# Two attentions with fewer waits, and the reciprocal of a block's sum moved behind the next block's maximum

## What is computed

```python
def one_block(qi):                       # 128 queries of one head against all 1024 keys
    s = jnp.einsum('bqkgd,bskd->bkgqs', qi, k, preferred_element_type=jnp.float32) * scale
    p = jax.nn.softmax(s, axis=-1)
    return jnp.einsum('bkgqs,bskd->bqkgd', p.astype(v.dtype), v)
```

```python
s = jnp.where(kpos[None, :] <= qpos[:, None], s, -jnp.inf)
prob = jax.nn.softmax(s, axis=-1)
outs.append(jnp.einsum('bhqk,bhkd->bhqd', prob.astype(v.dtype), v[:, :, :q1]))
```

## Time and profile before

| | us |
|---|---|
| median of 3 runs | 2623.56 |
| lowest and highest | 2619.59, 2625.0 |
| span of the profiled execution | 2619.9 |
| PE busy of the span | 2539.2 (97%) |
| DVE busy | 1587.0 (61%) |
| ACT busy | 1233.5 (47%) |
| POOL busy | 1132.0 (43%) |
| first attention, back of step 2 to back of step 62 | 188.07 |

### The profile page before, as it was taken

One profiled execution on the slowest core, in us unless ns is written; L12 is line 12 of the kernel. 1 busy time (PEld: TensorE's weight loads), 2 busy tenths in 40 slices (PEclk: granted clock), 3 DMA queues, 4 the chain that ended last, 5 costly groups with the idle time before them and its releaser, 6 DMA issues.

```text
span 2619.9 us, 33861 instructions
## 1 busy us (share of the span) xinstructions
PE 2539.2 (97%) x12946; PEld 2112.9 (81%) x12946; DVE 1587.0 (61%) x2413; ACT 1233.5 (47%) x1858; POOL 1132.0 (43%) x754
## 2 busy tenths in 40 slices
PE   5999999999999999999999999999999999999998
PEld 3788788777888888878788888888888888888886
DVE  7654889578555566575833366666666666655333
ACT  4343888445444443333533345543656656652132
POOL 0222434437878774444487334233322222235233
PEclk8999999999999999999999999999999999999999
DMA  6134000432222126553233322222111111157342
GB/s 271 65 121 129 1 1 1 142 101 83 94 77 92 73 100 226 192 177 109 107 113 121 121 73 89 81 69 93 57 53 53 49 49 57 60 206 279 146 185 97
DMA packets 84465, 275.89 MB, mean 105 GB/s; under 512 B 9392, under 2 KB 9520, under 8 KB 84304
## 3 DMA queue, kind: packets, MB, share of 16 engines
q1 hardware_dynamic: 84304, 273.71, 29.8%
HBM read 219.54 MB, written 54.13 MB: 104 GB/s over the span
## 4 chain that ended last, share of the span: by engine, by line
PE 81%; DVE 10%; ACT 5%; issue 2%; POOL 1%; DMA 0%; DVEq 0%; SPq 0%; ACTq 0%; POOLq 0%
PE ps L609 12%; PE ps L611 11%; PE ps L610 11%; PE ps L977 7%; PE ps L978 7%; PE ps L979 7%; PE ps L848 5%; PE ps L829 4%; PE ps L1034 3%; PE ps L1036 3%; PE ps L1035 3%; DVE wf L3047 2%; PE ps L805 2%; PE ps L806 2%; DVE st L2573 1%
## 5 line engine op out<-in xcount | busy, mean ns | idle before, releaser
L3374 POOL TENSOR_TENSOR hl<-raw,hl 128x1024 fp32r<-128x1024 f32 x161 | 403.6, 2509 | 929.9 <-ACT hl L1393 929.9
L609 PE MATMUL ps<-ht,hl 128*128 128x512 f32 x1552 | 633.7, 408 | 10.5 <-DVE ht L2444 5.4
L611 PE MATMUL ps<-ht,hl 128*128 128x512 f32 x1552 | 608.4, 392 | 0.0
L610 PE MATMUL ps<-ht,hl 128*128 128x512 f32 x1552 | 608.2, 392 | 0.0
L609 PEld LDWEIGHTS ps<-ht,hl 128*128 128x128 f32 x1552 | 293.6, 189 | 71.3 <-issue 6.2
L611 PEld LDWEIGHTS ps<-ht,hl 128*128 128x128 f32 x1552 | 293.0, 189 | 63.7
L610 PEld LDWEIGHTS ps<-ht,hl 128*128 128x128 f32 x1552 | 294.0, 189 | 54.2 <-issue 1.7
L3451 POOL TENSOR_SCALAR wf<-wf,st 128x1024 f32<-128x1024 f32 (+2 forms) x192 | 167.9, 874 | 343.1 <-DVE st L2581 287.4
L1393 ACT ACTIVATE hl<-raw 128x1024 fp32r<-128x1024 f32 x163 | 171.4, 1053 | 182.2 <-PE ps L1036 66.5
L2384 DVE TENSOR_TENSOR ps<-ps,wf 128x512 f32<-128x512 f32 x116 | 80.8, 697 | 152.1 <-PE ps L979 151.9
L829 PEld LDWEIGHTS ps<-cst,wf 128*128 128x128 f32 x1088 | 126.6, 141 | 56.2 <-issue 34.4
(11 more groups left out here) (287 smaller groups left out, 5298.5 us busy)
## 6 DMA issues: line engine op xcount, KB each, us to landing
raw<-in_wst SPq DMA_DIRECT2D x243, 512.0 KB, 4.0
wf<-scratch_rows SPq DMA_DIRECT2D x32, 512.0 KB, 5.0
scratch_g<-wf SPq DMA_DIRECT2D x22, 512.0 KB, 2.6
wf<-scratch_g SPq DMA_DIRECT2D x44, 256.0 KB, 4.4
wf<-in_xT SPq DMA_DIRECT2D x16, 512.0 KB, 8.0
htf<-in_wst SPq DMA_DIRECT2D x16, 512.0 KB, 15.4
scratch_ys<-wr SPq DMA_DIRECT2D x16, 512.0 KB, 4.8
ht<-scratch_ys SPq DMA_DIRECT2D x32, 256.0 KB, 6.0
```

The lines of the kernel that those rows point to most:

```text
L609: self.op.matmul(out, wh, xh[:, c], start=(j == 0), stop=False)
L610: self.op.matmul(out, wh, xl[:, c], start=False, stop=False)
L611: t = self.op.matmul(out, wl, xh[:, c], start=False, stop=(j == kt - 1))
L3374: self.op.tensor_tensor(K.hl[:, u * 2048 + 1024:u * 2048 + 2048], K.raw[:, i % 3 * 1024:(i % 3 + 1) * 1024], hi.bitcast(F32), ALU.subtract ...
```

## The change

- DVE, first attention: in step s the order top(s+2), turn(s), soft(s+2), back becomes top(s+2), soft(s+1), turn(s), back. The reciprocal of block s+1 is thus issued one step later than before, behind the maximum of block s+2.
- PE, first attention: in scores(s+2), from s = 0 on, the last of the four matmuls gets a wait for `weighed` of block s. turn(s), which follows, waits for the same label already.
- Waits left out in both attentions, since another wait that stays, or the new one, includes them: on PE `top` ahead of the scores (first attention) and `phi` ahead of turn and back; on ACT `top` (causal) or `scores` (first), the first half of `turn` of block g-4, and `weighed` of block g-16; on DVE `exp` of block g-16, `weighed` of block g-16 and `turn` ahead of the low part; on POOL `exp` ahead of weigh.

```diff
--- before.py
+++ after.py
@@ -790,7 +790,7 @@
         self.last_tails()
         self.mark("stage", "project1")
 
-    def scores(self, A, g, h, qt, q, kh, kl, causal, ready):
+    def scores(self, A, g, h, qt, q, kh, kl, causal, ready, weighed=None):
         K = self.K
         nk = (qt + 1) * 128 if causal else 1024
         pair = g % 2
@@ -803,6 +803,8 @@
             for label in ready:
                 self.wait_ge(*K.at(*label))
             self.op.matmul(out, qs, K.wrr(kh)[:, c], start=True, stop=False)
+            if c.stop == nk and weighed is not None:
+                self.wait_ge(*K.at("weighed", A, weighed))
             t = self.op.matmul(out, qs, K.wrr(kl)[:, c], start=False, stop=not diag)
             if diag:
                 self.consts()
@@ -810,7 +812,7 @@
                 t = self.op.matmul(K.ps[pair][:, nk - 128:nk], K.idr[:, :], K.maskr[:, :],
                                    start=False, stop=True)
         t.then_inc(*self.done("scores", A, g))
-        free = (("top", A, g),) if causal else (("top", A, g), ("exp", A, g))
+        free = (("top", A, g),) if causal else (("exp", A, g),)
         for half in range((nk + 511) // 512):
             self.emptied[2 * pair + half] = free
 
@@ -829,7 +831,7 @@
                 t = self.op.transpose(K.ps[2][:, o:o + 128], K.w(p)[:, j * 128:(j + 1) * 128],
                                       K.c_id)
             t.then_inc(*self.done("turn", A, g, half))
-            self.emptied[4 + bk] = (("phi", A, g, half), ("plo", A, g, half))
+            self.emptied[4 + bk] = (("plo", A, g, half),)
 
     def back(self, A, g, qt, hi, lo, v, causal, ready):
 
@@ -837,7 +839,6 @@
         nk = qt + 1 if causal else 8
         for gg in (g - 1, g):
             for half in range((((qt if gg == g else qt - 1) + 1 if causal else 8) + 3) // 4):
-                self.wait_ge(*K.at("phi", A, gg, half))
                 self.wait_ge(*K.at("plo", A, gg, half))
         for label in ready:
             self.wait_ge(*K.at(*label))
@@ -858,7 +859,7 @@
             h, qt = s // 8, s % 8
             k = 8 if h < 4 else 10
             self.scores(1, s, h, qt, h, k, k + 1, False, (("stacklo", "q", h // 2), ("stacklo", "q", 4),
-                         ("stackhi2", "q", 4, 1)))
+                         ("stackhi2", "q", 4, 1)), s - 2 if s >= 2 else None)
 
         for s in range(-2, 66):
             if s + 2 < 64:
@@ -1630,18 +1631,14 @@
         nk = (qt + 1) * 128 if causal else 1024
         m, den = (K.st[:, 4 * (g % 16) + j:4 * (g % 16) + j + 1] for j in range(2))
         pw = K.w(p)[:, 0:nk]
-        self.wait_ge(*K.at("top", A, g))
         if causal:
             self.wait_ge(*K.at("minus", A, g))
         else:
-            self.wait_ge(*K.at("scores", A, g))
+            self.wait_ge(*K.at("top", A, g))
             if g >= 4:
-                for half in (0, 1):
-                    self.wait_ge(*K.at("turn", A, g - 4, half))
+                self.wait_ge(*K.at("turn", A, g - 4, 1))
             else:
                 self.wait_ge(*K.at("tok", 2 if g < 2 else 3))
-        if g >= 16:
-            self.wait_ge(*K.at("weighed", A, g - 16))
         self.op.activation(pw, pw if causal else K.ps[g % 2][:, 0:nk], ACT.Exp, bias=m, scale=1.0,
                            accum_out=den).then_inc(*self.done("exp", A, g))
 
@@ -2558,8 +2555,6 @@
         m = K.st[:, 4 * (g % 16):4 * (g % 16) + 1]
         ps = K.ps[g % 2][:, 0:nk]
         self.wait_ge(*K.at("scores", A, g))
-        if g >= 16:
-            self.wait_ge(*K.at("exp", A, g - 16))
         if causal:
             pw = K.w(p)[:, 0:nk]
             if g >= 3:
@@ -2591,7 +2584,6 @@
             src = v3(K.ps[2][:, bk * 512:bk * 512 + len(js) * 128])
             q = slice((qt % 2) * 128, (qt % 2) * 128 + 128)
             r = slice(js[0], js[-1] + 1)
-            self.wait_ge(*K.at("turn", A, g, half))
             self.wait_ge(*K.at("phi", A, g, half))
             self.op.tensor_tensor(lo[:, r, q], src, hif[:, r, q],
                                   ALU.subtract).then_inc(*self.done("plo", A, g, half))
@@ -2609,6 +2601,8 @@
         for s in range(-2, 66):
             if s + 2 < 64:
                 self.top(1, s + 2, (s + 2) // 8, (s + 2) % 8, 0, False)
+            if 0 <= s + 1 < 64:
+                self.soft(1, s + 1)
             if s == 40:
                 self.wait_ge(*K.at("toksq", 3))
                 self.copy_out(8, 1, 23, "tok")
@@ -2618,8 +2612,6 @@
                 self.att_square(slice(0, 768), 0)
             if 0 <= s < 64:
                 self.turn(1, s, s % 8, pt1(K, (s // 2) % 2), False)
-            if s + 2 < 64:
-                self.soft(1, s + 2)
             if s >= 2 and s % 2 == 0:
                 h = (s - 1) // 8
                 self.back(1, s - 1, h, (s - 1) % 8, K.htlf(4 + h // 2))
@@ -3446,7 +3438,6 @@
         nk = (qt + 1) * 128 if causal else 1024
         rd = K.st[:, 4 * (g % 16) + 2:4 * (g % 16) + 3]
         pw = K.w(p)[:, 0:nk]
-        self.wait_ge(*K.at("exp", A, g))
         self.wait_ge(*K.at("rd", A, g))
         self.op.tensor_scalar(pw, pw, rd, 0.0, ALU.mult,
                               ALU.add).then_inc(*self.done("weighed", A, g))
```

## The result

The changed kernel takes 2643.39 us (median of 4 runs, 2639.7 to 2646.61), the one before 2624.28 us in the same series: ratio 1.0077, 95% interval 1.006 to 1.0095, or 19 us slower. 2650.3 was forecast, with a range of 2638 to 2660.

The account below looks back on a forecast made before the run. The order of work on three nearly full engines, a two-step chain of 6.20 us per interval, was taken as the bound; 29 x 0.87 + 1.5 = 26.7 us on 2623.56 gave 2650.3 us, range 2638 to 2660.

Parts of the forecast that it names:

- Back to maximum 3.12: First attention, odd heads: from PE's back to DVE's next maximum, taken as unchanged at 3.12 us.
- maximum to reciprocal 1.26: DVE, first attention, odd heads: the moved reciprocal starts 1.26 us behind the maximum, as the low part did; even heads 1.14.
- Reciprocal to weighing 0.33: First attention: from DVE's reciprocal to POOL's start of weighing, taken as 0.33 us.
- the waits left out cost nothing: Both attentions: dropped waits were taken as worth 0 us, with a bound of 0 to -6.2 us in the second attention.
- Weighing 1.12: POOL, first attention: weighing of a block was taken to last 1.12 us, now on the interval's path.
- POOL's end to the matmul 0.14: First attention: from the end of weighing to PE's waiting last scores matmul, 0.14 us, taken from a wait for POOL elsewhere.
- Matmul to transposes 0.31: PE, first attention: from the last scores matmul, restarting an idle PE, to the transposes behind it, 0.31 us.
- transposes to back 0.79: PE, first attention: eight transposes to what follows, 0.79 us when nothing holds them.
- the one for which I gave none: First attention: the 7.34 us interval from 342.10 to 349.44, after a late exponential, was given no increase.
- the start: First attention, ahead of the first back: the new order was taken to add 1.5 us.
- the weighing did not stay covered: Rival, first attention: weighing stays covered and DVE's idle time is the gain, 2609 to 2623 us; chance 0.04.
- The clock did not fall: Rival: PE's idle time in each interval lowers the clock, costing 30 to 90 us, 2680 to 2740 us; chance 0.06.

Follow-up runs that it names:

- e7: The changed kernel with GpSimd's (POOL's) wait on the exponential put back ahead of weighing; ratio 1.0077 to the kernel before.
- e10: The kernel e2 with PE's waits on `phi` put back in turn and back of both attentions; ratio 0.9995 to the kernel before.
- e11: The kernel before with the waits left out and nothing else, no moved reciprocal and no new PE wait; ratio 0.999 to the kernel before.
- e2: The changed kernel with the reciprocal back in its old place, waits left out and PE's new wait kept; ratio 0.9987 to the kernel before.
- e5: The kernel before with the back of a pair of blocks one step later on PE, ACT and VectorE; ratio 0.9993 to the kernel before.
- e12: The kernel before with back one step later and the waits left out, without PE's new wait; 2615.54 us, ratio 0.9969 to the kernel before.
- e9: The kernel before with back one step later, the waits left out and PE's new wait, reciprocal in its old place; ratio 1.0037 to the kernel before.
- e1: The kernel before with only the reciprocal moved behind the next maximum, all waits kept and no new PE wait; ratio 1.007 to the kernel before.
- e8: The changed kernel without PE's new wait, the move and all left-out waits staying; ratio 1.0039 to the kernel before.
- e6: The kernel before with only PE's new wait for the weighed block ahead of the last scores matmul; ratio 1.0 to the kernel before.

## Why the prediction was right

The direction, the mechanism and the place were right; the time was 7 us too long. Point by point, by its steps:

- *Back to maximum 3.12, maximum to reciprocal 1.26.* Measured 3.12 (373.64 to 376.76) and 1.26 (376.76 to 378.02). In even heads it is 1.15 (285.62 to 286.77). The hold that the low part had in odd heads went over to the reciprocal, as the Trainium skill's rule ("VectorE: DVE Perf Modes", section "Two Vector instructions with no wait between them") has it. The trace agrees: the reciprocal starts 0.11 later in odd heads, and the low part right behind it follows 0.07 to 0.08 after its start in both.
- *Reciprocal to weighing 0.33.* Measured 0.26. The step that failed is "the waits left out cost nothing": GpSimd's wait on the exponential was worth 0.07, by e7.
- *Weighing 1.12.* Measured 1.12.
- *POOL's end to the matmul 0.14.* Measured 0.04 to 0.05. I took it from a matmul of the FFN stage that has more waits ahead of it (two weight tiles and its input). The low part's release shows the same two values, 0.14 and 0.04, with and without an earlier wait (e10, e11, e2), but that this is the reason in the FFN stage too is argued and not tested. 0.09 per interval.
- *Matmul to transposes 0.31, transposes to back 0.79.* Measured 0.34 and 0.79.

Together 6.94 in place of 7.07, 0.74 in place of 0.87: 29 x 0.13 is 3.8 us of the 7. The intervals with other work in them took less than a full increase: the one for which I gave none became 0.5 shorter (7.34 to 6.84), and four others (6.43, 6.40, 6.52 and the last, 6.20, before) rose by 0.4 rather than 0.74, another 1.3 us. So the intervals are 5.6 us below the sum (25.2 against 19.6), the start 0.4 (1.1 against 1.5) and the last interval 0.1. The second attention gained 1.6 where 0 was taken, within the bound of -6.2. That is 7.7 us, and 26.7 less 7.7 is the 19.0 that the trace shows. So the path was right, and what was mis-sized is the price of waits: two terms of the sum by the waits ahead of an instruction, and the second attention's, which was put at nothing.

The rivals: the weighing did not stay covered, though its minor part, a gain from waits, is real at 3 us. The clock did not fall in the repeating part: PE idles for 1.16 us in each interval and the granted clock is 1.00 in 275.7 to 483.4. It fell ahead of that and behind it. At the start of the kernel after it fell behind an idle time of 3.88 us (the busy times by stretches of PE, 270 to 274), and again at 493 to 497, to 0.63 and 0.50, behind three idle spells of PE between the last backs and the next stage. The kernel before has both falls too (270 to 274 and 470 to 475).

```profile
270.00:272.00 2.00, 0.95 (x5) 0.91 0.00 0
272.00:274.00 2.00, 2.00 (x8) 0.50 0.00 0
```

The length of an idle spell doesn't decide it alone. The kernels of before, e5 and e12 all idle 3.22 us at the start (until 268.48, 268.01 and 267.88). Before, the clock was at the lower level, 1.2 GHz, for about 3.4 us, from 270.0 on; in e5 for about 6.8 us, from 267.1 on, when PE was still idle; in e12 it stayed at 1.00 (its row for 268 to 270):

```profile
268.00:270.00 2.00, 1.97 (x12) 1.00 0.00 0
```

From the first scores matmul to the first back it is 16.8 us before and 17.6 to 17.7 in e2 and e11, whose clock was low for 6.8 us as well; with back one step later it is 19.1 in e5 and 17.2 in e12. At half the clock 3.4 us of work lose at most 1.7, my estimate from these stretches. With one trace of each kernel it stays open what decides how long the clock is low.

The page of the Trainium skill on short idles ("TensorE: Matmul & The Clock Gate", "A second HAM failure mode: psum-queue depth-cycling") would have had the clock swing here; the trace doesn't show it for idles of this length and spacing. One trace has a single fall within this stage: in e9 the granted clock is 0.62 and 0.53 in 348 to 352, behind idle spells of 1.03 and 0.45 us. The page of the Trainium skill on extra semaphore instructions ("Perfetto Trace Analysis", "Identifying Dependency Chains") was the better guide than my reading of the rows: the 1047 instructions and the 192 of e7 agree with it. It gives no price; e7 and e10 do, and I should not have set the price at zero for want of a row.

## What to carry to other kernels

Before an instruction is moved back in an engine's order, look for its reader's reader: a reciprocal of 0.16 us carried 1.1 us of weighing behind it, and 1.6 us of slack were gone with one place in the order. A wait moved forward to an earlier instruction is free as long as its label is there; once it is the last to come, the work between the two places waits with it (here 0.28 us per interval for one matmul). Put it as late in the order as the data allows. And look at chains of exactly equal length: moving one (e5) only shows the next, and here it took the order, the waits and the place of one wait together to gain 0.3%.

## What I had not expected of the hardware

A wait that has long been satisfied is not free when it stands ahead of the wait that comes last: 0.07 us between VectorE's reciprocal and GpSimd's start (0.33 with two waits, 0.26 with one, e7), and 0.10 us between VectorE's low part and TensorE's first transposes (0.14 in before, e10, e11 and e12, 0.04 in e2). Behind the late wait it cost nothing that shows (0.04 to 0.05 in e1 and e8), and neither did a satisfied wait ahead of an engine that is running on other work (e6). And around the same idle time of TensorE, 3.22 us, the clock was at the lower level for about 3.4 us in one kernel, for 6.8 in another and not at all in a third.
